# Attention values as split side-by-side tiles, query blocks in pairs, softmax one unit further ahead

## Chip, cores and metric

The program runs on one core of one Trainium2 chip. The metric is the device time of one execution in microseconds. Engines are named as in the profile: PE (matrix products), PEld (its weight loads), DVE, ACT, POOL, SP.

## What is computed

One hybrid layer (a gated MLP mixer, an attention called NSA with 16 heads in 4 groups of 64 columns, a recurrent mixer, a merge, a feed-forward part) on 512 rows of 1024, then two layers of another kind. The change lies in NSA, whose core is, for each head:

```python
s_c = einsum(q, kc) * scale; p_c = softmax(where(valid_c, s_c, NEG))      # compressed keys, 31
o_cmp = einsum(p_c, vc)
p   = softmax(where(kpos <= t, q @ k_slc * scale, NEG));  o_slc = p @ v_slc    # selected blocks
sw  = softmax(where(wmask, q @ k_win * scale, NEG));      o_win = sw @ v_win   # window of 512
o   = g[0] * o_cmp + g[1] * o_slc + g[2] * o_win         # g = sigmoid of 3 gates per head and query
```

With 512 rows there are 8 blocks of 64 and the top 16 are asked for, so that every block is selected, and the window of 512 covers everything: both branches are causal attention over 512 keys, with keys and values of their own. Then `o` is multiplied by a weight matrix.

## The kernel before

All projections are products in fp32r, each operand split into a high part (rounded) and a low part (the rest), with three products of 512 or 280 columns for each pair of tiles. ACT makes the high half of a weight panel (`split_hi`), DVE the low half (`split_lo`); SP loads the next panel when `w_lo` says that the old one was split.

Attention runs over *units*. `unit(u)` gives, for head k = u // 6, six units v = u % 6 (96 in all; k runs over 16 heads): the query block `qb` of 128 rows, the first branch `b` and how many branches `n` (selected, window). v0 is block 0 with both branches, v1 block 1 with both, v2 and v3 block 2 with one branch each, v4 and v5 block 3 with one branch each. A unit goes through:

- `scores(u)` on PE: query block by keys, high and low part (fp32r), and the causal mask by a bf16 product, into bank 4 + u % 2; it waits until the exp of unit u - 2 is done.
- `maxima(u)` on DVE, `exps(u)` on ACT with the row sums (an exp and a read of the accumulator for each branch), `factor(u)` on DVE (reciprocal, times gate), and on POOL (L600) the multiplication of the probabilities `Pn` by that factor; three buffers.
- `transposes(u)` on PE (L2310), one for each 128 keys and branch, into bank 6; the copy to `PTn` by ACT for even u (L981), by DVE for odd u (L1627).
- `values(u)` on PE: for each branch and key block a product of the whole value tile `Vt` (128 columns, two groups of 64, plain fp32, two instructions a product) with 128 columns of `PTn`, added in bank 7. Only the 64 rows of the unit's own group are used. The first unit of a head starts its rows with the compressed branch (31 rows by 512 columns).
- After the sixth unit ACT makes the high part of the output (`o_hi`, L958) and DVE the low part (`o_lo`), from bank 7.

The order is written out by hand. In step u PE does `scores(u + 2)`, some matmuls of the next projection (`fill`, the panel `gmlp_v`, 192 matmuls in all, 52 before the loop and nine a head in it), `transposes(u)`, more `fill`, `values(u - 1)`. ACT does `exps(u + 2)`, for even u the copy, for v0 `o_hi` of the head before; DVE `maxima(u + 2)`, `factor(u + 1)`, for odd u the copy, for v0 `o_lo`. The splits of the filler's weights stand in the same queues, at units found by `slot_after` (1, 30, 62 and 94 or one to two later). All queues are in order. All products are recorded on line 2076 (`mm`).

## Time and profile before

| | before |
|---|---|
| median of 3 runs | 2606.17 us (2605.89 to 2609.31) |
| profiled execution | 2610.13 us, span 2608.5 us |
| PE busy | 2563.4 us (98%), 12825 instructions |
| PEld busy | 2136.6 us (82%) |
| DVE busy | 1201.1 us (46%) |
| ACT busy | 924.1 us (35%) |
| POOL busy | 404.4 us (16%) |
| chain that ended last | PE 92%, DVE 4%, ACT 2%, POOL 1%, DMA 1% |
| granted PE clock | 0.997 of full |

Times in the rows are microseconds from the span's start, or ns where it says mean. In a timeline a row is one or more instructions of a kind in a row: start, length from the first start to the last end, engine, line, operation, output<-inputs, shapes and count; at the end, in brackets, idle time of the engine before it and who ended it. PE overlaps its instructions, so the time that one costs is read from start to start. The loop of the attention runs from 186 to about 407 us.

### The profile page before, as it was taken

The numbers are of one execution on the slowest core, as the hardware profiler recorded it, in microseconds if no ns is written. First come the engines' busy times: TensorE is split into PE (matmuls) and PEld (weight loads), VectorE is DVE, ScalarE is ACT, GpSimd is POOL, SyncE is SP. The second block draws the span as 40 slices with busy tenths as digits, with TensorE's granted clock in tenths as the row PEclk, the third lists the DMA queues.
The fourth block names the chain that finished last, engine by engine and source line by source line (L and its number), as shares of the span: only waits on it lengthen the run. The fifth ranks groups of instructions, "written<-read, shape, count | busy, mean of one in ns | idle before, by whom it ended". The sixth has DMA issues, their size and how long they took to land.

```text
span 2608.5 us, 31776 instructions
## 1 busy us (share of the span) xinstructions
PE 2563.4 (98%) x12825; PEld 2136.6 (82%) x12825; DVE 1201.1 (46%) x1665; ACT 924.1 (35%) x1316; POOL 404.4 (16%) x426
## 2 busy tenths in 40 slices
PE   8999999999999999999999999999999999999998
PEld 7877778887888888888888888888888888888886
DVE  5445553645544574464523333443452333443435
ACT  6435454226323422122533333223253433223232
POOL 2103332300000010000301001321012111022300
PEclk9999999999999999999999999999999999999999
DMA  5220002232242364452233232222223222322231
GB/s 210 81 83 15 17 17 93 97 101 81 81 178 97 127 210 159 150 193 81 81 113 113 97 103 97 87 92 81 97 77 117 97 97 89 127 87 86 88 104 65
DMA packets 58205, 265.49 MB, mean 102 GB/s; under 512 B 5385, under 2 KB 21905, under 8 KB 32865
## 3 DMA queue, kind: packets, MB, share of 16 engines
q1 hardware_dynamic: 46672, 223.39, 25.0%
q0 software_dynamic: 11120, 39.27, 4.3%
q8 instruction: 92, 1.51, 0.2%
q10 hardware_dynamic: 288, 1.05, 0.1%
q14 instruction: 33, 0.26, 0.0%
HBM read 261.60 MB, written 2.10 MB: 101 GB/s over the span
## 4 chain that ended last, share of the span: by engine, by line
PE 92%; DVE 4%; ACT 2%; POOL 1%; DMA 1%; issue 1%; DVEq 0%; SPq 0%; ACTq 0%
PE PS L2076 89%; DVE w_split L1273 1%; PE PS L2310 1%; ACT w_split L699 1%; POOL merged L600 1%; DMA raw<-in_weights 1%; DVE small L1580 1%; PE PS L2498 1%; PE PS L2165 0%; DVE ks_lo L1514 0%; DVE xres L1343 0%; PE PS L2576 0%; ACT merged L878 0%; ACT merged L877 0%; DVE xres L2031 0%
## 5 line engine op out<-in xcount | busy, mean ns | idle before, releaser
L2076 PE MATMUL PS<-h_act,w_split 128*128 128x512 f32 (+1 forms) x5856 | 1268.4, 377 | 12.9 <-DVE w_split L1273 3.9
L2076 PEld LDWEIGHTS PS<-h_act,w_split 128*128 128x128 f32 x5856 | 1048.5, 189 | 214.1 <-DVE w_split L1273 4.7
L1273 DVE TENSOR_TENSOR w_split<-raw,w_split 128x2048 fp32r<-128x2048 f32 x209 | 502.2, 2403 | 832.9 <-ACT w_split L699 819.1
L699 ACT ACTIVATE w_split<-raw 128x2048 fp32r<-128x2048 f32 x209 | 400.2, 1915 | 888.6 <-PE PS L2076 880.3
L2076 PE MATMUL PS<-w_split,h_act 128*128 128x512 f32 (+1 forms) x1920 | 454.4, 387 | 4.5 <-DVE w_split L1273 3.3
L2076 PEld LDWEIGHTS PS<-w_split,h_act 128*128 128x128 f32 x1920 | 349.4, 189 | 67.6 <-DVE w_split L1273 4.3
L2076 PE MATMUL PS<-y_act,w_split 128*128 128x512 f32 x1152 | 263.4, 389 | 0.0
L2076 PEld LDWEIGHTS PS<-y_act,w_split 128*128 128x128 f32 x1152 | 216.3, 188 | 44.9
L2076 PE MATMUL PS<-w_split,y_act 128*128 128x512 f32 x528 | 132.0, 398 | 0.4 <-DVE w_split L1273 0.4
L2076 PE MATMUL PS<-R 128*128 128x128 f32 (+3 forms) x576 | 128.0, 368 | 0.0
L600 POOL TENSOR_TENSOR merged<-merged,small 128x256 f32<-128x256 f32 (+2 forms) x96 | 88.2, 918 | 209.6 <-DVE small L1589 209.2
L2076 PEld LDWEIGHTS PS<-R 128*128 128x128 f32 x576 | 92.4, 191 | 25.3 <-issue 13.9
L2076 PEld LDWEIGHTS PS<-w_split,y_act 128*128 128x128 f32 x528 | 95.5, 188 | 17.7 <-DVE w_split L1273 0.8
L662 POOL TENSOR_TENSOR merged<-merged,cm 128x128 f32<-128x128 f32 (+2 forms) x24 | 41.7, 1764 | 411.0 <-DVE cm L1913 411.0
L950 ACT ACTIVATE merged<-PS,small 128x128 f32<-128x128 f32 (+3 forms) x128 | 66.9, 525 | 108.7 <-DVE small L1580 108.6
L804 ACT ACTIVATE stage<-PS 128x512 f32<-128x512 f32 x94 | 55.9, 598 | 136.8 <-PE PS L2076 136.7
L1580 DVE TENSOR_REDUCE small<-PS 128x2 f32<-128x256 f32 (+2 forms) x96 | 57.7, 601 | 69.8 <-PE PS L2076 69.6
L2076 PE MATMUL PS<-w_split,res_hi 128*128 128x512 f32 x256 | 79.0, 390 | 0.0
L655 POOL TENSOR_TENSOR res_hi<-h_act,cf 128x512 fp32r<-128x512 f32 x16 | 24.5, 1532 | 251.5 <-DVE h_act L1281 251.5
L2076 PEld LDWEIGHTS PS<-merged,R 128*128 128x128 f32 x432 | 53.2, 191 | 7.5 <-issue 6.8
L2076 PE MATMUL PS<-merged,R 128*128 128x128 f32 x432 | 58.6, 278 | 0.1
L2310 PE MATMUL PS<-cf,merged 128*128 128x128 f32 x320 | 51.5, 275 | 6.5 <-POOL merged L600 4.6
(310 smaller groups left out, 2052.6 us busy)
## 6 DMA issues: line engine op xcount, KB each, us to landing
raw<-in_weights SPq DMA_DIRECT2D x197, 1024.0 KB, 4.8
R<-in_w_ada POOLq DMA_DIRECT2D x36, 512.0 KB, 4.9
raw<-in_weights SPq DMA_DIRECT2D x18, 512.0 KB, 4.9
gate_bc<-in_w_ada POOLq DMA_DIRECT2D x12, 512.0 KB, 4.7
raw<-in_weights SPq DMA_DIRECT2D x16, 256.0 KB, 3.6
R<-in_nsa_wk POOLq DMA_DIRECT2D x1, 2048.0 KB, 12.0
xres<-in_x POOLq DMA_DIRECT2D x1, 2048.0 KB, 10.2
R<-in_decay POOLq DMA_DIRECT2D x8, 256.0 KB, 3.3
```

Of the source, the lines that this page charges most:

```text
L600: pool.tensor_tensor(probs, probs, nsa_fac[:, u % 4, 0:n].unsqueeze(2).to_broadcast([P, n, nk]), ALU.mult).then_inc(p_ready, 1)
L655: pool.tensor_tensor(residue_tiles[part][kt].rearrange("p (r i) -> p r i", r=RES), source, ones, ALU.mult).then_inc(residues_ready, 1)
L662: pool.tensor_tensor(probs, probs, share.unsqueeze(2).to_broadcast(list(probs.shape)), ALU.mult).then_inc(a_p, 1)
L699: act.activation(w_split[:, 0, half, :, :], raw[:, half, :, :], ACT.Copy).then_inc(w_hi, 1)
L804: act.activation(stage[:, slot0 + j, :], PS[:, 4 * S + j, :], func).then_inc(staged, 1)
L950: last = act.activation(Pn[:, u % 3, k * nk:(k + 1) * nk], PS[:, 4 + u % 2, k * nk:(k + 1) * nk], ACT.Exp, bias=nsa_nmx[:, u % 4, k:k + 1] ...
L1273: dve.tensor_tensor(w_split[:, 1, half, :, :], raw[:, half, :, :], w_split[:, 0, half, :, :].bitcast(F32), ALU.subtract).then_inc(w_lo, 1)
L1580: dve.reduce_max(nsa_nmx[:, u % 4, 0:n], PS[:, 4 + u % 2, 0:n * (qb + 1) * P] .rearrange("p (b k) -> p b k", b=n), AX, negate=True).then_i ...
L2076: return pe.matmul(out, lhsT, rhs, start=start, stop=stop, skip_group_check=True)
L2310: last = pe.transpose(PS[:, 6, k * P:(k + 1) * P], Pn[:, u % 3, k * P:(k + 1) * P], ident)
L2498: last = pe.transpose(PS[:, 4 * S + b, k * P:(k + 1) * P], tile, ident)
```

## The change

- The unit order within a head becomes block 0, block 1, block 2 branch 0, block 3 branch 0, block 2 branch 1, block 3 branch 1. Units are taken in pairs of query blocks: `chunk(u)` lists which blocks of probabilities of the pair are transposed at step u and which products follow. A product now covers one or two query blocks (128 or 256 columns).
- The stationary value tile holds, for one group and branch, the high half and the low half of the values side by side (64 + 64 columns, fp32r). ACT makes the high, DVE (first group pair) or POOL (second) the low halves.
- The transposed probabilities are split too: ACT makes the high part of every unit (`pt_hi`), DVE the low part (`pt_lo`), from banks 6 and 3 in turn. Each product runs twice, with the high and with the low part.
- Both halves of bank 7 now belong to the same head: ACT copies the other half (`o_other`), DVE adds (`o_sums`), ACT makes the high part (`o_hi`), POOL the low part (`o_lo`). The compressed product fills all 128 rows of bank 7 (its values are padded with zeros to 128 columns) and waits for that sum.
- Scores, maxima and exps run three units ahead instead of two, the factor two instead of one, with a fourth buffer of probabilities. Transposes of even units wait for both units of their pair.
- The filler uses banks 0, 1, 2, 0 and the staggered order; its first weight half is free after 72 of 96 matmuls instead of 48.

The diff, cut to this:

```diff
-    qb, b, n = ((0, 0, 2), (1, 0, 2), (2, 0, 1), (2, 1, 1), (3, 0, 1), (3, 1, 1))[v]
+    qb, b, n = ((0, 0, 2), (1, 0, 2), (2, 0, 1), (3, 0, 1), (2, 1, 1), (3, 1, 1))[v]
...
+def chunk(u):
+    v = u % 6
+    if v == 0:
+        return ([Block(k, (k + 1) * P * b) for b in range(2) for k in range(2)],
+                [Product(0, b, 0, 2, 2 * P * b) for b in range(2)])
+    if v == 1:
+        return [Block(1, 2 * P * b + P) for b in range(2)], [Product(1, b, 1, 2, P * b) for b in range(2)]
+    b = v // 2 - 1
+    if v % 2 == 0:
+        return ([Block(k, P * kb) for kb in range(2) for k in range(2)],
+                [Product(kb, b, 2, 4, 2 * P * kb) for kb in range(2)])
+    return ([Block(0, 2 * P), Block(1, 2 * P), Block(1, 3 * P)], [Product(2, b, 2, 4, 0), Product(3, b, 3, 4, 2 * P)])
...
-assert slot_after(FILL_SIZE // 2 * 3 + 12) > UNITS // 2
+FILL_BANKS = (0, 1, 2, 0)
+FILL_TILE_DONE = (36, 48, 84, 96)
+FILL_HALF_DONE = 72
+assert slot_after(FILL_SIZE + FILL_TILE_DONE[0]) > UNITS // 2 + 1
...
+        def pt_tile(u, part):
+            if u % 2 == 0:
+                return pt_even[:, part, :]
+            return y_act[:, part, 2, :] if u // 6 < 4 else pt_late[:, part, :]
...
+        def v_parts(tiles, g, part):
+            return tiles.rearrange("p t (b g a n) -> p t b g a n", b=2, g=2, a=2)[:, :, :, g, part ^ g, :]
+        def v_both(gp, kb, b, g):
+            tile = V0_pairs[kb // 2][:, kb % 2, :] if gp == 0 else V1_all[:, kb, :]
+            return tile[:, (2 * b + g) * P:(2 * b + g + 1) * P]
...
+                pool.wait_ge(p_ready, products)
+                pool.wait_ge(hi_made, at("att").h + k + 1)
+                rows = slice(64 * (k % 2), 64 * (k % 2) + 64)
+                lo = y_act[rows, 1, k // 2, :]
+                pool.tensor_tensor(lo, y_sum[rows, k // 2, :], y_act[rows, 0, k // 2, :].bitcast(F32), ALU.subtract
+                                   ).then_inc(act_lo, 1)
+                pool.wait_ge(act_lo, at("att").l + k + 1)
             for u in range(UNITS):
                 gp, hp, g, qb, b, n = unit(u)
                 nk = (qb + 1) * P
                 pool.wait_ge(fac_ready, u + 1)
-                probs = Pn[:, u % 3, 0:n * nk].rearrange("p (b k) -> p b k", b=n)
+                probs = probs_tile(u)[:, 0:n * nk].rearrange("p (b k) -> p b k", b=n)
                 pool.tensor_tensor(probs, probs, nsa_fac[:, u % 4, 0:n].unsqueeze(2).to_broadcast([P, n, nk]), ALU.mult
                                    ).then_inc(p_ready, 1)
+                if u % 6 == 4 and u > 6:
+                    o_lo(u // 6 - 1, u + 1)
+                if u == UNITS // 2 - 1:
+                    for g in range(2):
+                        pool.wait_ge(v_ready, 8 + g)
+                        src = Vt1.rearrange("p t (b g n) -> p t b g n", b=2, g=2)[:, :, :, g, :]
+                        pool.tensor_tensor(v_parts(V1_all, g, 1), src, v_parts(V1_all, g, 0).bitcast(F32),
+                                           ALU.subtract).then_inc(v_lo, 1)
+            o_lo(4 * HPG - 1, UNITS)
...
-                act.activation(Vt[gp], banks[:, :, 0:256], ACT.Copy).then_inc(v_ready, 1)
+                if gp == 0:
+                    for t in range(2):
+                        for g in range(2):
+                            src = banks[:, 2 * t:2 * t + 2, 0:256].rearrange("p t (b g n) -> p t b g n", b=2, g=2)
+                            act.activation(v_parts(V0_pairs[t], g, 0), src[:, :, :, g, :], ACT.Copy
+                                           ).then_inc(v_ready, 1)
+                else:
+                    act.activation(Vt1, banks[:, :, 0:256], ACT.Copy).then_inc(v_ready, 1)
                 act.activation(gS[:, gp], banks[:, :, 256:280], ACT.Sigmoid).then_inc(v_ready, 1)
-                release(S, v_ready, 2 * gp + 2)
+                if gp == 1:
+                    release(S, v_ready, 7)
                 split_hi(c.g + 1, 1)
...
-                if u >= 3:
-                    act.wait_ge(t_ready, u - 2)
+                if u >= 4:
+                    act.wait_ge(t_ready, 2 * ((u - 4) // 2) + 2)
                 for k in range(n):
-                    last = act.activation(Pn[:, u % 3, k * nk:(k + 1) * nk], PS[:, 4 + u % 2, k * nk:(k + 1) * nk],
+                    last = act.activation(probs_tile(u)[:, k * nk:(k + 1) * nk], PS[:, 4 + u % 2, k * nk:(k + 1) * nk],
                                           ACT.Exp, bias=nsa_nmx[:, u % 4, k:k + 1],
                                           accum_out=nsa_sum[:, u % 4, k:k + 1])
...
+            def o_other(k):
+                act.wait_ge(o_ps, k + 1)
+                rows, other = [slice(64 * (x % 2), 64 * (x % 2) + 64) for x in (k, k + 1)]
+                act.activation(y_sum[rows, k // 2, :], PS[other, 7, :], ACT.Copy).then_inc(o_part, 1)
             def o_hi(k):
-                act.wait_ge(o_ps, k + 1)
+                act.wait_ge(o_sum, k + 1)
                 rows = slice(64 * (k % 2), 64 * (k % 2) + 64)
-                act.activation(y_act[rows, 0, k // 2, :], PS[rows, 7, :], ACT.Copy).then_inc(hi_made, 1)
+                act.activation(y_act[rows, 0, k // 2, :], y_sum[rows, k // 2, :], ACT.Copy
+                               ).then_inc(hi_made, 1)
+            def pt_hi(u):
+                act.wait_ge(t_ready, u + 1)
+                cols = P * len(chunk(u)[0])
+                act.activation(pt_tile(u, 0)[:, 0:cols], PS[:, (6, 3)[u % 2], 0:cols], ACT.Copy).then_inc(pt_act, 1)
...
-            for u in range(UNITS + 2):
+            exps(2)
+            for u in range(UNITS + 3):
                 if u < UNITS:
-                    gp, hp, g, qb, b, n = unit(u)
-                    if u + 2 < UNITS:
-                        exps(u + 2)
-                    if u % 2 == 0:
-                        act.wait_ge(t_ready, u + 1)
-                        cols = n * (qb + 1) * P
-                        act.activation(PTn[:, u % 2, 0:cols], PS[:, 6, 0:cols], ACT.Copy).then_inc(pt_act, 1)
-                    if u % 6 == 0 and u:
-                        o_hi(u // 6 - 1)
-                if u == UNITS:
-                    o_hi(4 * HPG - 1)
+                    pt_hi(u)
+                    if u + 3 < UNITS:
+                        exps(u + 3)
+                if u % 6 == 0 and 0 < u <= UNITS:
+                    o_other(u // 6 - 1)
+                if u % 6 == 1 and 1 < u:
+                    o_hi(u // 6 - 1)
+                if u == UNITS // 2 - 5:
+                    for g in range(2):
+                        src = Vt1.rearrange("p t (b g n) -> p t b g n", b=2, g=2)[:, :, :, g, :]
+                        act.activation(v_parts(V1_all, g, 0), src, ACT.Copy).then_inc(v_ready, 1)
                 for f in range(FILL_GROUPS):
-                    if u == slot_after(FILL_SIZE * f + FILL_SIZE // 2):
+                    if u == slot_after(FILL_SIZE * f + FILL_HALF_DONE):
                         split_hi(at("gmlp_v").g + f + 1, 0)
                     for j in range(4):
-                        if u == slot_after(FILL_SIZE * f + FILL_SIZE // 2 + 12 * (j + 1)):
+                        if u == slot_after(FILL_SIZE * f + FILL_TILE_DONE[j]):
                             fill_tile(f, j)
                     if u == slot_after(FILL_SIZE * (f + 1)) + 1:
                         split_hi(at("gmlp_v").g + f + 1, 1)
...
-            for gp in range(2):
-                skip(at("nsa.v", gp))
+            c = at("nsa.v", 0)
+            split_lo(c.g + 1, 0)
+            dve.wait_ge(v_ready, 5)
+            for t in range(2):
+                for g in range(2):
+                    src = PS[:, 2 * t:2 * t + 2, 0:256].rearrange("p t (b g n) -> p t b g n", b=2, g=2)
+                    dve.tensor_tensor(v_parts(V0_pairs[t], g, 1), src[:, :, :, g, :],
+                                      v_parts(V0_pairs[t], g, 0).bitcast(F32), ALU.subtract).then_inc(v_lo, 1)
+            release(0, v_lo, 4)
+            split_lo(c.g + 1, 1)
+            skip(at("nsa.v", 1))
...
-            def o_lo(k):
-                dve.wait_ge(hi_made, c.h + k + 1)
+            def o_sums(k):
+                dve.wait_ge(o_part, k + 1)
                 rows = slice(64 * (k % 2), 64 * (k % 2) + 64)
-                low(y_act[rows, 1, k // 2, :], PS[rows, 7, :], y_act[rows, 0, k // 2, :])
+                both = y_sum[rows, k // 2, :]
+                dve.tensor_tensor(both, PS[rows, 7, :], both, ALU.add).then_inc(o_sum, 1)
+            def pt_lo(u):
+                dve.wait_ge(pt_act, u + 1)
+                cols = P * len(chunk(u)[0])
+                dve.tensor_tensor(pt_tile(u, 1)[:, 0:cols], PS[:, (6, 3)[u % 2], 0:cols],
+                                  pt_tile(u, 0)[:, 0:cols].bitcast(F32), ALU.subtract).then_inc(pt_dve, 1)
...
+            maxima(2)
+            factor(1)
             for u in range(UNITS + 3):
+                if u + 3 < UNITS:
+                    maxima(u + 3)
+                if u % 6 == 1 and 1 < u:
+                    o_sums(u // 6 - 1)
+                if u + 2 < UNITS:
+                    factor(u + 2)
                 if u < UNITS:
-                    gp, hp, g, qb, b, n = unit(u)
-                    if u + 2 < UNITS:
-                        maxima(u + 2)
-                    if u + 1 < UNITS:
-                        factor(u + 1)
-                    if u % 2 == 1:
-                        dve.wait_ge(t_ready, u + 1)
-                        cols = n * (qb + 1) * P
-                        dve.tensor_copy(PTn[:, u % 2, 0:cols], PS[:, 6, 0:cols]).then_inc(pt_dve, 1)
-                    if u % 6 == 0 and u:
-                        o_lo(u // 6 - 1)
-                if u == UNITS:
-                    o_lo(4 * HPG - 1)
+                    pt_lo(u)
                 for f in range(FILL_GROUPS):
-                    if u == slot_after(FILL_SIZE * f + FILL_SIZE // 2) + 1:
+                    if u == slot_after(FILL_SIZE * f + FILL_HALF_DONE) + 1:
                         split_lo(at("gmlp_v").g + f + 1, 0)
                     if u == slot_after(FILL_SIZE * (f + 1)) + 2:
                         split_lo(at("gmlp_v").g + f + 1, 1)
...
-                        out = PS[:, 4 * S + bank0 + j, 0:width]
+                        out = PS[:, 4 * S + bank0 + banks[j], 0:width]
+                        if first and j in begin:
+                            begin[j]()
...
-                    yield from dense(at("gmlp_v").plus(C(g=n, u0=n)), 0, Hr, feat=False)
+                    yield from dense(at("gmlp_v").plus(C(g=n, u0=n)), 0, Hr, feat=False, stagger=True, banks=FILL_BANKS,
+                                     begin={3: lambda: pe.wait_ge(gv_raw, 4 * n + 1)})
...
-            def transposed(u):
-                pe.wait_ge(pt_dve if u % 2 else pt_act, u // 2 + 1)
             def transposes(u):
-                gp, hp, g, qb, b, n = unit(u)
-                pe.wait_ge(p_ready, u + 1)
-                if u:
-                    transposed(u - 1)
-                else:
+                pe.wait_ge(p_ready, u // 2 * 2 + 2)
+                if u == 0:
                     pe.wait_ge(pct_act, 4)
-                for k in range(n * (qb + 1)):
-                    last = pe.transpose(PS[:, 6, k * P:(k + 1) * P], Pn[:, u % 3, k * P:(k + 1) * P], ident)
+                blocks = chunk(u)[0]
+                for k, block in enumerate(blocks):
+                    last = pe.transpose(PS[:, (6, 3)[u % 2], k * P:(k + 1) * P],
+                                        probs_tile(u // 2 * 2 + block.unit)[:, block.col:block.col + P], ident)
                 last.then_inc(t_ready, 1)
...
-                gp, hp, g, qb, b, n = unit(u)
+                gp, hp, g = unit(u)[0:3]
                 if u % 6 == 0:
                     rows = slice(32 * hp, 32 * hp + NCMP)
-                    mm(PS[64 * g:64 * g + 64, 7, :], vc[rows, 2 * gp + g, :], PcT[2 * gp + g][rows, :], True, False)
                     if u:
-                        pe.wait_ge(act_lo, att.l + u // 6)
-                transposed(u)
-                nk = (qb + 1) * P
-                for k in range(n):
-                    for kb in range(qb + 1):
-                        last = mm(PS[:, 7, qb * P:(qb + 1) * P], Vt[gp][:, kb, (b + k) * P:(b + k + 1) * P],
-                                  PTn[:, u % 2, k * nk + kb * P:k * nk + (kb + 1) * P], False, True)
+                        pe.wait_ge(o_sum, u // 6)
+                    mm(PS[:, 7, :], vc[rows, 2 * gp + g, :], PcT[2 * gp + g][rows, :], True, False)
+                if u % (UNITS // 2) == 0:
+                    pe.wait_ge(v_lo, 4 + 2 * gp)
+                pe.wait_ge(pt_dve, u + 1)
+                for x in chunk(u)[1]:
+                    n = (x.q1 - x.q0) * P
+                    for part in range(2):
+                        last = mm(PS[:, 7, x.q0 * P:x.q1 * P], v_both(gp, x.kb, x.b, g),
+                                  pt_tile(u, part)[:, x.col:x.col + n], False, True)
                 if u % 6 == 5:
                     last.then_inc(o_ps, 1)
...
+            scores(2)
             for u in range(UNITS):
-                if u + 2 < UNITS:
-                    scores(u + 2)
+                if u + 3 < UNITS:
+                    scores(u + 3)
                 fill((FILL[u] + 1) // 2)
                 transposes(u)
                 fill(FILL[u] // 2)
```

## Rows read from the trace of the kernel before

**Rows 1.** View of windows, the attention: window, length, busy (instructions) of PE, PEld, DVE, ACT, POOL
```profile
186.00:409.00 223.00, 215.85 (x1505) 172.03 (x1504) 125.02 (x351) 112.38 (x324) 88.39 (x97) 1.00 0.05 15
```

**Rows 2.** Timeline of PE in one head: start, length, engine, line, operation, count
```profile
236.10 0.30 PE L2076 MATMUL PS<-ks_hi,qs 128*128 128x128 f32 x1
...
244.38 1.07 PE L2076 MATMUL PS<-R,merged 31*64 31x512 f32 x2
...
245.37 0.71 PE L2076 MATMUL PS<-merged,R 128*128 128x128 f32 x4
...
245.84 0.48 PE L2076 MATMUL PS<-ks_hi,qs 128*128 128x512 f32 x1
...
246.43 0.48 PE L2076 MATMUL PS<-w_split,h_act 128*128 128x512 f32 x1
...
246.75 0.49 PE L2310 MATMUL PS<-cf,merged 128*128 128x128 f32 x3
...
249.72 0.30 PE L2076 MATMUL PS<-ks_hi,qs 128*128 128x128 f32 x1
...
250.29 0.48 PE L2076 MATMUL PS<-w_split,h_act 128*128 128x512 f32 x1
...
250.84 0.66 PE L2310 MATMUL PS<-cf,merged 128*128 128x128 f32 x4
...
251.34 0.83 PE L2076 MATMUL PS<-merged,R 128*128 128x128 f32 x6
...
251.92 0.36 PE L2076 MATMUL PS<-ks_hi,qs 128*128 128x256 f32 x1
...
252.13 0.28 PE L2076 MATMUL PS<-ks_lo,qs 128*128 128x256 f32 x1
...
252.24 0.28 PE L2076 MATMUL PS<-ks_hi,qs 128*128 128x256 f32 x1
```

**Rows 3.** Timeline of ACT, DVE and POOL in the same head
```profile
239.91 0.47 ACT L950 ACTIVATE merged<-PS,small 128x256 f32<-128x256 f32 x1 [1.25 <-DVE small L1580]
...
240.73 0.20 ACT L950 ACTIVATION_READ_ACCUMULATOR merged<-PS,small 128x1 f32 x1
...
246.66 0.69 DVE L1580 TENSOR_REDUCE small<-PS 128x1 f32<-128x512 f32 x1 [0.90 <-PE PS L2076]
...
247.39 0.69 ACT L950 ACTIVATE merged<-PS,small 128x512 f32<-128x512 f32 x1 [1.91 <-DVE small L1580]
...
247.70 0.83 POOL L600 TENSOR_TENSOR merged<-merged,small 128x384 f32<-128x384 f32 x1 [1.63 <-DVE small L1589]
...
247.97 0.19 ACT L950 ACTIVATION_READ_ACCUMULATOR merged<-PS,small 128x1 f32 x1
...
248.71 0.69 DVE L1580 TENSOR_REDUCE small<-PS 128x1 f32<-128x512 f32 x1 [1.09 <-PE PS L2076]
...
249.32 0.15 DVE L1588 RECIPROCAL small<-small 128x1 f32<-128x1 f32 x1
...
249.75 1.04 POOL L600 TENSOR_TENSOR merged<-merged,small 128x512 f32<-128x512 f32 x1 [1.22 <-DVE small L1589]
```

**Rows 4.** Groups by line and form, 186 to 409 us: count, busy, mean ns
```profile
L1281 DVE TENSOR_TENSOR y_act<-PS,y_act 64x512 fp32r<-64x512 f32 x15 | 10.3, 688 | 22.3 <-ACT y_act L958 22.3
...
L981 ACT ACTIVATE merged<-PS 128x512 f32<-128x512 f32 x16 | 9.5, 595 | 0.8 <-PE PS L2310 0.8
```

**Rows 5.** Views of two lines on POOL: shortest, median, longest ns
```profile
L675 POOL TENSOR_TENSOR R<-R x16: 1277/1288/1293, 1598.8 to 2439.7; 128x512 f32<-128x512 f32 x16
...
L677 POOL TENSOR_TENSOR R<-R x16: 1277/2309/3341, 1600.0 to 2440.9; 128x512 f32<-128x512 f32 x16
```

**Rows 6.** Timeline around a weight split inside a head
```profile
259.57 2.54 DVE L1273 TENSOR_TENSOR w_split<-raw,w_split 128x2048 fp32r<-128x2048 f32 x1
...
264.99 0.31 PE L2076 MATMUL PS<-ks_hi,qs 128*128 128x128 f32 x1
```

**Rows 7.** Timeline of PE in the last group ahead of the attention
```profile
147.66 1.55 PE L2076 MATMUL PS<-w_split,h_act 128*128 128x280 f32 x10 [0.96 <-DVE w_split L1273]
```

46 lines of the change are left out of this document (35 added, 11 removed).

## The prediction, made before the changed kernel was built

> **What bounds the kernel now.** The page first: TensorE (PE) is busy for 98% of the span, so only a stretch in which PE has work taken away or is made to wait can change the time. The change touches one stretch, the attention from about 186 to 409 us, and the last weight group ahead of it. The view of windows [rows 1] shows 215.9 us of PE busy in those 223, DVE 125, ACT 112, POOL 88: PE is the bound on average, but this kernel hands every unit through all four engines, so the averages don't decide. I therefore read the timeline of one head (six units, v0 to v5) by the starts of its instructions, since PE's durations overlap. The scores of unit v0 start at 236.10 and again at 249.72 [rows 2]: a head takes 13.62 us. At one place PE is already late: between the projection matmul at 250.29 and the transposes at 250.84 lie 0.55 us, where the same matmul is followed after 0.32 us at 246.43 [rows 2]; 0.23 us of waiting for the probabilities that POOL finishes at 250.79 [rows 3]. So PE's own work in a head is 13.39 us, and the softmax chain stands right behind it.
>
> **What the edit takes from PE.** The values of a head are now 20 products of 128 columns, each of two fp32 instructions; six of these take 0.58 us (251.34 to 251.92), 0.10 each, so 4.0 us a head. After the change they are 24 fp32r instructions of 128 or 256 columns, in blocks of four. The scores show their price: the first of a block 0.21 us, the next 0.11 (251.92, 252.13, 252.24) [rows 2]. Six blocks of 0.21 + 3 x 0.11 make 3.2 us. The compressed product, 0.99 us now (244.38 to 245.37), keeps its 512 fp32 columns; a stationary tile twice as wide is not shown, I bound it by 0.99 and 1.10 and take 1.05. PE's work falls by 0.75 us to about 12.6 us a head. If nothing else counted, 15 heads would give 15 us.
>
> **What it adds to the others.** Per head, with the durations of [rows 4]: ACT converts six transposed tiles instead of copying three (0.60 us for 512 columns) and copies the other 64 rows of the output (taken as the same 0.60). DVE subtracts six tiles (0.69 for 512 columns) instead of copying three, and adds instead of subtracting at the head's end. POOL takes over the low half of the output. Its nearest row is a two-input operation on 512 elements, 1.28 us [rows 5]; its lower bound is the multiplication with a broadcast factor, 1.04 [rows 3]. I take 1.28. In totals the engines still have room (ACT about 8 of 13.6 us, DVE about 9.5, POOL about 7). The question is the order in each queue.
>
> **The chain after the change.** Prices [rows 2 to 4]: transposes of four blocks are readable 0.66 us after their start; ACT starts 0.04 later; an activation lets the next start 0.11 before its end (the accumulator read starts at 247.97, 0.58 into an exp of 0.69), so 0.49 for a copy of 512 and 0.68 for exp of 512; two exps of 256 with their reads last 1.02 (239.91 to 240.93); DVE's maximum starts 0.23 after the scores' block ends (246.43 to 246.66) and lets the next start after 0.61 (248.71 to 249.32); POOL starts 0.43 after the factor's first step (249.32 to 249.75), which I write as 0.35 + 0.08, multiplies for 1.04 (0.83 for 384 columns), PE starts 0.05 later. In the new queues ACT converts transpose u *before* the exps of u+3, DVE takes the maximum of u+3, then (in v1) the output's sum, then the factor of u+2, then the low part of u; even transposes wait for both units of their pair. This closes three links, in time from the transposes of v4:
> - to the transposes of the next v0, which need p(v1): 0.66 + 0.04 + 0.49 (conversion) + 1.02 (exps of v1) = 2.21. DVE is by then still on the low part of v4 (1.34 to 1.94) and the maximum of v2 (to 2.42). Then 0.35 + 0.08 + 1.04 + 0.05 = 3.94. PE's own work up to there is 3.64.
> - on to the values of v0, which overwrite the whole of bank 7 and so wait for the sum of the previous head: 0.70 + 0.49 + 0.68 (exps of v3, ahead in ACT's queue) + 0.60 (other half) + 0.07 (DVE still on the maximum of v4) + 0.69 (sum) + 0.05 = 3.28. PE's own work: 2.86. Before, the compressed product did not have to wait for this; now it stands behind the wait, with everything behind it.
> - on to the transposes of v4, which need p(v5): 1.05 + 0.56 (values v0) + 0.59 (scores of v5, 245.84 to 246.43) + 0.22 + 0.61 (maximum v5, in front of the factor of v4) + 0.35 + 0.08 + 0.83 (p(v4)) + 0.07 + 1.28 (low half of the output, in front of p(v5) on POOL) + 0.07 + 1.04 + 0.05 = 6.80. Without the low half there it would be 6.28, PE's own work being 6.21.
>
> Sum: 3.94 + 3.28 + 6.80 = 14.02 us a head, against 13.62. The 0.75 us freed on PE turn into 1.4 us of waiting. Looking one unit further ahead does not help, because it is ACT's and DVE's queue that hold the next unit back, not the scores.
>
> **The rest of the sum.** Fifteen heads x 0.40 = +6.0. A head in which DVE splits a weight half (2.54 us in its queue) took 264.99 - 249.72 = 15.27, 1.65 more than the others [rows 6]; two such heads lie in the old loop, the third split falling into its first units. In the new order of the filler (half 0 free only after 72 of 96 matmuls) it falls at unit 13, in the running loop: +1.65. POOL's two low parts of the second value pair (2 x 1.28) stand before p(48) and p(49), which are needed later than that: 0 to 2, I take +0.5. In the group ahead of the attention PE already waits 0.96 us for DVE's second half [rows 7]; ACT's four value copies instead of one stand in front of that: 0 to 1, I take +0.5. DVE's four value subtractions there lie beside ACT's own 1.9 us split, at nothing; without that cover they would cost 1.8. The drain gets one hand-over more (conversion, then low part): +0.7. The start, with one unit more in flight but no split in it, -0.4. Sum: 6.0 + 1.65 + 0.5 + 0.5 + 0.7 - 0.4 = +9 us. The profiled execution took 2610.1 us (span 2608.5); it becomes 2619. It is 4 us above the median of the runs, 2606.2, which becomes 2615. A measurement of this kernel can tell about 0.2%, 5.2 us, from no change.
>
> **The rivals.**
> 1. *The chain is shorter than PE's work* (the other side). It decides from 12.6 us a head, that is if 1.4 us of the 14.02 are not there: if DVE and ACT come to each step at once. For it: two of the three links exceed PE's work by under 0.5 us, and their sums use in-order waits that I placed by hand. Against it: the old loop already waits 0.23 us on the same chain with only half the conversions. Then 15 x (12.65 - 13.62) = -14.5, and +2 for the rest: 2593.
> 2. *Only POOL's addition is off*: if the low half finds a gap (an earlier factor for v4), the third link is 6.28 and a head 13.5: 15 x -0.12 = -2, with +3 for the rest: 2607.
> 3. *Splits cost double.* [Rows 5]: the same POOL operation of 512 elements takes 1.28 us in one line and 2.31 (up to 3.34) in the line right behind it, so something beside it can hold POOL up. If each of the three splits also stops POOL's new work, the head loses its 2.3 us and POOL's 1.3: three times +2 more, with some more for the value parts: 2622. The Trainium skill ("SBUF — State Buffer", Who interferes with whom) says that a VectorE instruction with two SBUF inputs and a GpSimd instruction that reads SBUF shut each other out for their whole length. By it the weight split (both inputs in SBUF) is such a partner and the new subtractions from PSUM are not; the sum of this rival comes out of it, that of the forecast is without it. The trace has the long durations, but does not show whose they are.
> 4. *The change doesn't do what it says*: the wide stationary tile loads slower than the narrower shapes of [rows 2], so that PE keeps its 13.4 us of work. The chain still decides, and with PE closer behind it a head is 14.2: 2618.
>
> **How the numbers follow.** Forecast 0.41 (2611 to 2619), rival 1 0.18 (2587 to 2600), rival 2 0.28 (2601 to 2611), rival 3 0.10 (2619 to 2626), rival 4 0.03. Faster by over 0.2% (under 2601): rival 1 and the low end of 2, 0.20. Slower (over 2611.4): forecast, 3 and 4, less 0.04 at the forecast's low end, 0.50. Within: 0.30. The range, 2594 to 2622, leaves out half of rival 1 and half of rival 3, 0.14. It holds the bounds of the prices: 1.04 instead of 1.28 for POOL's addition takes 15 x 0.24 = 3.6 off, the unknown value parts move it by 2.
>
> **What would show it.** In the profile after: values as blocks of four at 0.21/0.11; a head of about 14.0 us; PE idle before the transposes of v0 (0.3) and v4 (0.6), put down to POOL, and before the compressed product (0.4), put down to DVE's sum; POOL's low half between p(v4) and p(v5); three heads of 15.6. A head of 12.6 without waits proves rival 1, one of 13.5 with the wait at v4 gone rival 2. It would be wrong altogether if a 256-column fp32r product in these blocks did not take 0.11, or if the waits stood at other units than these.

## The result and the profile after

The changed kernel takes 2621.7 us (median of four runs, 2619.0 to 2623.0) against 2606.8 for the kernel before, run beside it (2605.9 to 2609.3): a ratio of 1.0052, 95% interval 1.0039 to 1.0064. It is slower, by more than the 0.2% that can be told. The profiled execution took 2623.0 us, its span 2621.4 against 2608.5, so +12.9 where +9 was forecast.

Busy times of the changed kernel, then the view of windows for the attention (columns as in [rows 1]):

```profile
PE 2549.5 (97%) x12569; PEld 2114.4 (81%) x12569; DVE 1235.8 (47%) x1717; ACT 957.1 (37%) x1385; POOL 430.5 (16%) x445
...
186.00:409.00 223.00, 192.41 (x1200) 143.03 (x1199) 152.00 (x387) 138.60 (x378) 105.31 (x108) 0.98 0.04 15
```

Beside [rows 1], in the same 223 us, the other three engines are busier (DVE 152 instead of 125, ACT 139 instead of 112, POOL 105 instead of 88), and PE stands idle for 30.6 us instead of 7.2. The same stretch of the clock isn't the same work, though: after it the changed kernel still has 11 us of attention to do. Up to the first matmul of the next dense part (407.63 us before the change, 420.49 after it) the windows are, before and after:

```profile
186.00:407.63 221.63, 214.48 (x1500) 170.86 (x1498) 123.65 (x351) 111.78 (x323) 87.56 (x95) 1.00 0.05 15
...
186.00:420.49 234.49, 199.64 (x1245) 148.26 (x1244) 157.58 (x399) 144.25 (x388) 109.49 (x112) 0.99 0.04 14
```

For the same work PE is busy for 199.6 us instead of 214.5, so the values did get cheaper, and idle for 34.9 instead of 7.2. The waits from 186 to 430 us name who it waits for (engine, line, tile, releaser: total us, number, longest; the PEld rows are the waits of the weight loads, which run ahead of the products):

```profile
PEld PS L2426 <- POOL merged L678: 15.9, 16, 3.2
...
PEld PS L2426 <- POOL R L678: 12.2, 12, 1.8
PE PS L2426 <- POOL merged L678: 10.8, 15, 2.9
PE PS L2195 <- DVE y_sum L1711: 9.2, 15, 0.6
PE PS L2426 <- POOL R L678: 8.5, 12, 1.6
```

L2426 is the transposes, waiting for POOL's probabilities; L2195 here is the compressed product, waiting for the output sum of the previous head, once a head for 0.6 us. One head on PE's timeline, from the transposes of v4 to the next ones, shows the three waits of the forecast, each at its place:

```profile
242.76 0.33 PE L2426 MATMUL PS<-cf,merged 128*128 128x128 f32 x1 [0.74 <-POOL R L678]
...
246.69 0.66 PE L2426 MATMUL PS<-cf,merged 128*128 128x128 f32 x4 [0.29 <-POOL merged L678]
...
250.04 1.12 PE L2195 MATMUL PS<-R,merged 31*128 31x512 f32 x2 [0.62 <-DVE y_sum L1711]
251.09 0.74 PE L2195 MATMUL PS<-pt_even,v_early 128*128 128x256 f32 x4
251.67 0.40 PE L2195 MATMUL PS<-ks_hi,qs 128*128 128x512 f32 x1
...
256.89 0.66 PE L2426 MATMUL PS<-cf,merged 128*128 128x128 f32 x4 [0.75 <-POOL merged L678]
```

The links are 246.69 - 242.76 = 3.93 us, 3.35 and 6.85, together 14.13. Without the three waits (0.29, 0.62 and 0.75 us) PE's own work in this head is 12.46 us. The same head on POOL and DVE:

```profile
240.22 1.28 POOL L669 TENSOR_TENSOR y_act<-y_sum,y_act 64x512 fp32r<-64x512 f32 x1
241.67 1.04 POOL L678 TENSOR_TENSOR R<-R,small 128x512 f32<-128x512 f32 x1 [0.16 <-DVE small L1705]
...
239.08 0.16 DVE L1705 TENSOR_TENSOR small<-small,R 128x1 f32<-128x1 f32 x1
...
240.77 0.76 DVE L1705 TENSOR_TENSOR small<-small,R 128x1 f32<-128x1 f32 x1
```

L669 is the low half of the output, in POOL's queue ahead of p(v5), as foreseen. Not foreseen is DVE's factor beside it: one number a row, 0.16 us in the unit before, here 0.76. It ends at 241.53, when L669 ends (241.50).

The starts of v0's scores give all heads of the trace: 13.45, 14.12, **18.55**, 14.12, 14.25, **15.75**, 14.11, 14.39, five of 14.11 to 14.13, **15.76**. The three in bold hold a weight split on DVE. The last two cost 1.63 and 1.64 us, as forecast, the first 4.43. There, on DVE and POOL, and PE afterwards:

```profile
221.70 2.28 DVE L1380 TENSOR_TENSOR w_split<-raw,w_split 128x2048 fp32r<-128x2048 f32 x1
...
224.42 0.70 DVE L1705 TENSOR_TENSOR small<-small,R 128x1 f32<-128x1 f32 x1
...
221.69 3.42 POOL L669 TENSOR_TENSOR y_act<-y_sum,y_act 64x512 fp32r<-64x512 f32 x1
225.26 1.04 POOL L678 TENSOR_TENSOR merged<-merged,small 128x512 f32<-128x512 f32 x1 [0.16 <-DVE small L1705]
```

```profile
219.60:226.30 6.70, 3.87 (x32) 3.31 (x30) 6.07 (x12) 3.13 (x9) 5.28 (x3) 0.98 0.16 35
226.30:232.70 6.40, 6.34 (x25) 5.15 (x26) 2.74 (x7) 2.56 (x8) 1.66 (x3) 0.50 0.31 129
232.70:239.10 6.40, 5.81 (x35) 4.04 (x33) 3.56 (x12) 3.40 (x9) 1.87 (x2) 0.99 0.00 0
```

The low half starts beside the split and ends at 225.11: it takes 2.14 us more than its own 1.28, nearly the whole length of the split (2.28). PE then waits 2.9 us (the longest wait above), and for the next 6.4 us its granted clock is 0.50, that is 1.2 GHz instead of 2.4.

The time lost, part by part. Both traces start the same transposes at 181.25, so that they can be laid on each other from there:

- the start, up to the second head's first scores: 14.30 us before, 11.84 now, -2.5 (before the change the first split stood here, and PE waited 1.59 us behind it);
- 14 heads at 0.50 more: +7.0;
- what stands out of the row of heads (the splits, the low parts of the second values), 7.4 us now against 2.9 before: +4.5;
- the drain, from the last head's first scores to the next dense part: 18.51 us before (389.12 to 407.63), 22.30 now (398.19 to 420.49), +3.8;
- behind the drain the clock is at 0.50 for about 3 us, in the dense part: +1.6.

That is 14.4 us in all; the same matmuls of the dense part behind lie 14.46 us apart in the two traces. The span grew by only 12.9 because 1.5 us come back around 1250 us, far behind the change; experiment 9's trace gains the same 1.5 us there, so it is the trace of the kernel before that is slow at that place. The drain, with the four waits that make it longer:

```profile
413.49 0.74 PE L2195 MATMUL PS<-pt_even,v_both 128*128 128x256 f32 x4 [0.66 <-DVE pt_even L1716]
...
415.86 0.33 PE L2426 MATMUL PS<-cf,merged 128*128 128x128 f32 x1 [1.62 <-POOL R L678]
...
417.93 0.74 PE L2195 MATMUL PS<-pt_even,v_both 128*128 128x256 f32 x4 [0.66 <-DVE pt_even L1716]
...
419.97 0.68 PE L2195 MATMUL PS<-pt_late,v_both 128*128 128x256 f32 x4 [1.31 <-DVE pt_late L1716]
...
421.00:424.00 3.00, 3.00 (x9) 2.35 (x8) 1.81 (x2) 0.90 (x2) 0.36 (x1) 0.51 0.28 44
```

### The profile page after: what moved, and what is told of

Same layout as the page of the kernel before. It is cut to its first block, busy times and chain, and to the rows that moved or that the text cites. A ratio compares the mean times of both kernels' runs of the same rounds, so it can differ in the third digit from the quotient of the medians.

```text
span 2621.4 us, 31327 instructions
## 1 busy us (share of the span) xinstructions
PE 2549.5 (97%) x12569; PEld 2114.4 (81%) x12569; DVE 1235.8 (47%) x1717; ACT 957.1 (37%) x1385; POOL 430.5 (16%) x445
## 3 DMA queue, kind: packets, MB, share of 16 engines
q10 hardware_dynamic: 288, 1.05, 0.1%
## 4 chain that ended last, share of the span: by engine, by line
PE 88%; DVE 5%; ACT 3%; issue 2%; POOL 1%; DMA 1%; DVEq 0%; SPq 0%; POOLq 0%; ACTq 0%
PE PS L2195 85%; DVE w_split L1380 1%; PE PS L2426 1%; POOL merged L678 1%; ACT pt_even L1064 1%; ACT w_split L786 1%; DVE small L1705 1%; DVE small L1696 1%; DMA raw<-in_weights 1%; PE PS L2618 0%; POOL R L678 0%; DVE y_sum L1711 0%; ACT y_sum L1053 0%; PE PS L2286 0%; DVE ks_lo L1621 0%
## 5 line engine op out<-in xcount | busy, mean ns | idle before, releaser
L2195 PE MATMUL PS<-h_act,w_split 128*128 128x512 f32 (+1 forms) x5856 | 1269.6, 377 | 12.2 <-DVE w_split L1380 3.1
L2195 PEld LDWEIGHTS PS<-h_act,w_split 128*128 128x128 f32 x5856 | 1049.4, 189 | 213.8 <-issue 4.9
L2195 PE MATMUL PS<-w_split,h_act 128*128 128x512 f32 (+1 forms) x1920 | 455.3, 388 | 3.9 <-DVE w_split L1380 2.9
L2195 PEld LDWEIGHTS PS<-w_split,h_act 128*128 128x128 f32 x1920 | 350.3, 189 | 67.0 <-DVE w_split L1380 4.0
L2195 PE MATMUL PS<-y_act,w_split 128*128 128x512 f32 x1152 | 263.4, 389 | 0.0
L2195 PEld LDWEIGHTS PS<-y_act,w_split 128*128 128x128 f32 x1152 | 216.2, 188 | 44.9
L2195 PE MATMUL PS<-w_split,y_act 128*128 128x512 f32 x528 | 132.0, 398 | 0.4 <-DVE w_split L1380 0.4
L2195 PE MATMUL PS<-R 128*128 128x128 f32 (+3 forms) x576 | 128.0, 368 | 0.0
L2195 PEld LDWEIGHTS PS<-R 128*128 128x128 f32 x576 | 92.4, 191 | 25.3 <-issue 13.9
L2195 PEld LDWEIGHTS PS<-w_split,y_act 128*128 128x128 f32 x528 | 95.5, 188 | 17.7 <-DVE w_split L1380 0.8
L678 POOL TENSOR_TENSOR merged<-merged,small 128x384 f32<-128x384 f32 (+2 forms) x72 | 61.3, 852 | 158.8 <-DVE small L1705 158.6
L2195 PE MATMUL PS<-w_split,res_hi 128*128 128x512 f32 x256 | 79.0, 390 | 0.0
L1696 DVE TENSOR_REDUCE small<-PS 128x1 f32<-128x384 f32 (+1 forms) x96 | 57.1, 595 | 28.2 <-PE PS L2195 26.8
L2426 PE MATMUL PS<-cf,merged 128*128 128x128 f32 x224 | 44.1, 285 | 20.5 <-POOL merged L678 10.8
L723 POOL DMA_DIRECT2D R<-in_w_ada x36 | 19.1, 532 | 241.1 <-DVEq L1907 241.1
L1246 ACT ACTIVATE R<-PS 128x512 f32<-128x512 f32 x48 | 28.7, 598 | 79.8 <-PE PS L2195 79.8
L1064 ACT ACTIVATE pt_even<-PS 128x512 fp32r<-128x512 f32 x48 | 28.7, 598 | 79.7 <-PE PS L2426 79.7
```

The costliest lines, as they stand in the source:

```text
L678: pool.tensor_tensor(probs, probs, nsa_fac[:, u % 4, 0:n].unsqueeze(2).to_broadcast([P, n, nk]), ALU.mult).then_inc(p_ready, 1)
L1064: act.activation(pt_tile(u, 0)[:, 0:cols], PS[:, (6, 3)[u % 2], 0:cols], ACT.Copy).then_inc(pt_act, 1)
L1246: act.activation(dst, src, ACT.Copy, scale=scale).then_inc(qk_ready, 1)
L1696: dve.reduce_max(nsa_nmx[:, u % 4, 0:n], PS[:, 4 + u % 2, 0:n * (qb + 1) * P] .rearrange("p (b k) -> p b k", b=n), AX, negate=True).then_i ...
L2195: return pe.matmul(out, lhsT, rhs, start=start, stop=stop, skip_group_check=True)
L2426: last = pe.transpose(PS[:, (6, 3)[u % 2], k * P:(k + 1) * P], probs_tile(u // 2 * 2 + block.unit)[:, block.col:block.col + P], ident)
```

## The experiments

Each kernel is the changed kernel with the edit shown, unless it says otherwise. Head lengths are distances between starts of v0's scores in its trace.

**1. The low half of the output on GpSimd two units later.**

```
-                if u % 6 == 4 and u > 6:
-                    o_lo(u // 6 - 1, u + 1)
+                if u % 6 == 0 and u > 6:
+                    o_lo(u // 6 - 2, u + 1)
...
+            o_lo(4 * HPG - 2, UNITS)
             o_lo(4 * HPG - 1, UNITS)
```

> POOL makes the low half of the output one head later, behind the probabilities of v0, where POOL stands idle for 2 us, instead of between those of v4 and v5. Theory (the chain through the queues sets the head): the transposes of v4 no longer wait for it. In the changed kernel the factor of v5 was held from 240.93 to 241.53 and the transposes of v4 began at 242.76; without it 240.93 + 0.08 + 1.04 + 0.05 = 242.10, so a head of 14.12 - 0.66 = 13.5 us, and 15 x 0.66 = 9.9 us off the time. The head with the first weight split, 18.55 us, loses more, since low half and split no longer meet: 15.5 or less, another 2 us off. Together 2609 to 2611. Rival (PE's own work decides, or another queue has taken the bound): the head stays at 14.1 and only the split's head gets shorter, 2619.

Measured: 2610.3 us (2608.5 to 2619.6), ratio to the kernel before 1.0014 (1.0005 to 1.0024); heads of 13.52. In a head of this trace the wait at v4 is gone, the other two stand:

```profile
345.09 0.33 PE L2427 MATMUL PS<-cf,merged 128*128 128x128 f32 x1 [0.34 <-POOL R L678]
...
348.45 1.12 PE L2196 MATMUL PS<-R,merged 31*128 31x512 f32 x2 [0.60 <-DVE y_sum L1712]
```

One position in one queue is worth 0.60 us a head, and 11.4 us of the 14.9 lost: 9 in the heads, and 2 in the head of the first split (16.54 instead of 18.55), where the low half no longer lies beside it. The same trace shows a new event: at unit 47 the two low parts of the second values (2.51 us in POOL's queue) now lie close to a low half of the output. PE waits 1.87 us, and the clock is at 0.50 for some 13 us behind it; the heads there take 18.21 and 15.59. The profiled execution is the longest of ten (2619.6), and the others lie between 2608.5 and 2613.4. So this fall of the clock probably doesn't come in every execution; only the profiled one has a trace.

**2. The first halves' splits two units later.**

```
-                    if u == slot_after(FILL_SIZE * f + FILL_HALF_DONE):
+                    if u == slot_after(FILL_SIZE * f + FILL_HALF_DONE) + 2:
```

(on ScalarE, and the same + 2 on VectorE)

> The splits of the filler's first weight half stand two units later in ACT's and DVE's queue (at v3 and v4 instead of v1 and v2 for the first, v2 and v3 for the second); nothing else moves. Theory (DVE's split and POOL's low half of the output shut each other out when they meet, and the pause of 2.9 us on PE then costs the clock): the first split's head falls from 18.55 to about 15.8 us, as the other two have it (15.75), and PE's clock does not fall: 2.8 us off the time, 2618 to 2619. Rival (a split at this point of the loop costs 4.4 us because the loop has no slack left, whoever is beside it): the head stays between 17.5 and 19, no change. All other heads stay at 14.12.

Measured: 2622.2 us, ratio 1.0053 (1.0036 to 1.0070): nothing gained. Moving the split away from the low half does end the mutual hold-up (on POOL 1.28 us again, the head 17.41 instead of 18.55), but PE still waits 2.49 us and the clock still falls to 0.50, for about 3 us instead of 6.4. And the split of unit 30, a second half, which the edit doesn't touch, got dearer, a head of 17.96 instead of 15.75:

```profile
271.18 0.47 PE L2426 MATMUL PS<-cf,merged 128*128 128x128 f32 x1 [1.23 <-POOL R L678]
```

that is the same 1.23 us of idle time as in the changed kernel's trace, only that the clock fell behind it here, for 6.6 us, and not there:

```profile
271.00:277.60 6.60, 6.42 (x26) 5.23 (x27) 2.91 (x10) 2.56 (x8) 1.77 (x3) 0.51 0.02 7
```

So a stretch of the loop at half the clock costs some 2.2 us (17.96 - 15.75). And my theory, the hold-up, covers at most 1.1 of the first split's 4.4 us, since the low clock got shorter in the same run. An estimate of the 4.4: 1.6 for the split in DVE's queue, as in the other two heads, 2.2 for the clock (from the head of 17.96), and 0.6 left for the hold-up and whatever else is different at this unit.

**3. Exponentials ahead of the conversion on ScalarE.**

```
                 if u < UNITS:
-                    pt_hi(u)
                     if u + 3 < UNITS:
                         exps(u + 3)
+                    pt_hi(u)
```

> ACT takes the exps of unit u + 3 before it converts the transposes of u, instead of behind. Theory of the prediction, taken at its word (the second link is set by DVE too: the low part and the maximum stand in front of the output's sum): the exps come 1 us earlier but the conversions 0.1 to 0.2 later, and DVE reaches the factor of v1 and the output's sum at the same time as before; a head stays within 14.0 to 14.3, the time within 2618 to 2624. Rival (ACT's order alone holds the chain): the factor of v1 and the sum come 0.5 us earlier each, a head of 13.3, 12 us off, 2610.

Measured: 2659.5 us, ratio 1.0198 (1.0181 to 1.0215). Both expectations missed it; a head takes 17.0 us. The order that the prediction blames for the lack of lead is far better than its opposite. Waits from 300 to 400 us:

```profile
ACT merged L1045 <- DVE small L1696: 28.8, 22, 3.2
DVE pt_even L1716 <- ACT pt_even L1064: 20.6, 18, 1.3
ACT R L1045 <- DVE small L1696: 14.1, 8, 3.0
```

ACT now waits for the maxima of u+3 with the conversion of u behind them, DVE's low part waits for the conversion, and the values for both. And each head now holds a stall of 1.2 to 1.4 us ahead of the compressed product, behind which the clock is low:

```profile
342.00:346.00 4.00, 4.00 (x18) 3.16 (x17) 0.92 (x3) 1.02 (x3) 1.13 (x2) 0.57 0.02 4
```

**4. PE's work in the values halved** (the products with the low parts of the probabilities are left out; their conversion stays).

```
-                    for part in range(2):
+                    for part in range(1):
```

> The products with the low part of the probabilities are left out (12 of 24 products a head, half of the values' work on PE); the low parts are still made and waited for. Theory (chain): PE loses 12 x 0.11 = 1.3 us of work a head, but only the products of v0 lie in the chain, so that a head falls by 0.2 to 0.3 us only, to 13.8 to 13.9, 4 us off, 2617. Rival (PE's work decides): a head of 12.8, 20 us off, 2602.

Measured: 2616.6 us (2616.3 to 2622.2), ratio 1.0038 (1.0024 to 1.0052); head 13.88. Some 1.5 us of PE's work a head are gone (half of six blocks of 0.41 to 0.58) and 0.24 us come back, as the theory said: the head is not PE's. What PE no longer does it waits, for example 0.98 us at v4 instead of 0.75:

```profile
340.43 0.65 PE L2426 MATMUL PS<-cf,merged 128*128 128x128 f32 x4 [0.98 <-POOL merged L678]
```

**5. The splits in quarters**, one in each of four successive units, on ScalarE and VectorE.

```
+            def split_lo_part(g, half, q):
+                if q == 0:
+                    dve.wait_ge(w_hi, 2 * g + half + 1)
+                ins = dve.tensor_tensor(w_split[:, 1, half, q, :], raw[:, half, q, :],
+                                        w_split[:, 0, half, q, :].bitcast(F32), ALU.subtract)
+                if q == 3:
+                    ins.then_inc(w_lo, 1)
```

> The changed kernel, with the three weight splits that fall into the attention loop (2.28 us each on VectorE, and one operation on ScalarE) cut into four quarters that are issued in four successive units. Theory (a split costs because it stands whole in VectorE's queue, and the first one pushes TensorE into a stall of 2.9 us behind which its granted clock is 0.50 for 6.4 us): the quarters of 0.6 us fit into VectorE's idle times of 0.4 to 1.8 us, so the heads of 18.55, 15.75 and 15.76 us come down to 14.1 to 14.6, no stretch of the loop has the clock at 0.50, and the kernel takes 2621.7 - 4.2 - 2 x 1.4 = 2615 us. Rival (what matters is the sum of VectorE's work between two links, wherever it lies): four units are delayed by 0.6 us each, the three heads stay near 16, only the clock comes back, 2619.

Measured: 2621.3 us, ratio 1.0048 (1.0033 to 1.0064): the heads are on the rival's side. The first split's head falls to 16.24 but its neighbour rises to 14.68, the other two take 15.41 and 16.98. The clock doesn't come back either, against both expectations: behind a wait of 1.20 us in the first head and one of 1.31 in the last it is at 0.50 for some 3 us. A quarter alone would be some 0.6 us (2.28 / 4); the first three on DVE took 0.81, 0.88 and 1.41. The last line is POOL's product beside the third:

```profile
227.13 0.81 DVE L1399 TENSOR_TENSOR w_split<-raw,w_split 128x512 fp32r<-128x512 f32 x1
...
229.38 0.88 DVE L1399 TENSOR_TENSOR w_split<-raw,w_split 128x512 fp32r<-128x512 f32 x1
...
231.84 1.41 DVE L1399 TENSOR_TENSOR w_split<-raw,w_split 128x512 fp32r<-128x512 f32 x1
...
231.66 1.04 POOL L678 TENSOR_TENSOR merged<-merged,small 128x512 f32<-128x512 f32 x1 [1.95 <-DVE small L1726]
```

POOL's products around the three quarters end at 227.39, 229.71 and 232.70, and each quarter ends 0.55 us behind that (227.94, 230.26, 233.25), whenever it had started. So in this trace a quarter waits for the product beside it and then takes its own 0.55. DVE comes to a quarter 0.3 to 0.9 us after it has handed a factor to POOL, while POOL's product runs.

**6. The output sum earlier**: the copy ahead of the exponentials on ScalarE, the addition ahead of the maxima on VectorE.

```
                 if u < UNITS:
                     pt_hi(u)
-                    if u + 3 < UNITS:
-                        exps(u + 3)
                 if u % 6 == 0 and 0 < u <= UNITS:
                     o_other(u // 6 - 1)
+                if u + 3 < UNITS:
+                    exps(u + 3)
...
-                if u + 3 < UNITS:
-                    maxima(u + 3)
                 if u % 6 == 1 and 1 < u:
                     o_sums(u // 6 - 1)
+                if u + 3 < UNITS:
+                    maxima(u + 3)
```

> The changed kernel, with the summing of the two halves of a head's output issued earlier: on ScalarE the copy of the other half ahead of the exponentials of that unit instead of behind them, on VectorE the addition ahead of the maxima. Theory (the second link of the head's chain, from the transposes of v0' to its values, contains the exponentials that stand ahead of the copy): the idle time of 0.62 us before the compressed product goes, each head takes 13.5 us instead of 14.12, the kernel 2621.7 - 15 x 0.6 = 2612.7. Rival (the head is set by VectorE's and GpSimd's row of factors and probabilities, and the exponentials that now come 0.6 us later delay them by as much): the wait moves ahead of the transposes and the head stays at 14.1, 2621.

Measured: 2615.2 us, ratio 1.0029 (1.0018 to 1.0040). Heads of 13.46 and 13.55, as the theory said, and no wait is left ahead of the compressed product. Of the 9 us only 6.5 arrive, because the heads with splits lose some back (17.09, 16.30, 17.89); in each of them the clock falls to 0.50, in the last for 6.8 us, where the changed kernel's trace has it in the first alone.

**7. Four edits together**: 1, 5 and 6, and the low halves of the second values in units 44 and 45 instead of both in 47.

```
-                if u == UNITS // 2 - 1:
-                    for g in range(2):
+                for g in range(2):
+                    if u == UNITS // 2 - 4 + g:
                         pool.wait_ge(v_ready, 8 + g)
```

> Four edits together: the low half of a head's output on GpSimd two units later (as tried alone before: head 13.52, kernel 2610.3), the output sums issued earlier, the splits in quarters, and the low halves of the second values in two units with free time on GpSimd (units 44 and 45 instead of both in 47). Theory (each acts on another link of the chain, so that the gains add up): head 13.52 - 0.6 = 12.9, 15 x 0.6 = 9 less; splits 7 less; no clock at 0.50 within the loop; 2610.3 - 16 = 2594, faster than the kernel before by 0.5%. Rival (behind the waits TensorE's own work is longer than was counted, or a new wait takes the place of each that goes): head 13.4, 2603 to 2606, no difference to the kernel before that can be told.

Measured: 2600.1 us (2597.0 to 2601.5), ratio 0.9967 (0.9955 to 0.9979), faster than the kernel before. The gains of edits 1 and 6 add up: heads of 12.86 and 12.96. The splits' heads are still 13.62 and 13.56 (the first), 14.95 and 15.64, together 6 us, by which the forecast of 2594 was missed. In the last of them PE waits 1.55 us and the clock is at 0.50 for 3.4 us, which the theory had ruled out.

**8. One part undone: the low half of the output on VectorE**, behind the low parts of v1', as before the change.

```
-                if u % 6 == 4 and u > 6:
-                    o_lo(u // 6 - 1, u + 1)
...
+                if u % 6 == 1 and 1 < u:
+                    o_lo(u // 6 - 1)
```

(the first on GpSimd, the second on VectorE)

> The changed kernel, with one part undone: the low half of a head's output is made on VectorE again, behind the low parts of the probabilities of v1', instead of on GpSimd between the products p(v4) and p(v5). Theory (the 1.28 us on GpSimd between the two products is the term of the second and third link, and VectorE is idle for 1.5 us at the place where the step now goes): the idle times before the transposes of v0' and v4 shrink as they did when the step stayed on GpSimd two units later, the head takes 13.5 us, the kernel 2610 to 2612. Rival (the step needs both of its inputs from SBUF, and shuts VectorE and GpSimd out from each other wherever it runs): it takes 1.3 to 1.8 us on VectorE, the factor behind it comes late, head 13.9 to 14.1, 2617 to 2621.

Measured: 2610.5 us (2607.1 to 2612.5), ratio 1.0012 (1.0003 to 1.0021); heads of 13.46, as short as in experiment 1. It takes 1.13 us on DVE in twelve of sixteen heads, with POOL's product beside it (0.69 in the others), in a gap, and costs nothing there:

```profile
344.63 1.13 DVE L1376 TENSOR_TENSOR y_act<-y_sum,y_act 64x512 fp32r<-64x512 f32 x1 [0.20 <-ACT y_act L1046]
...
346.25 0.69 DVE L1684 TENSOR_REDUCE small<-PS 128x1 f32<-128x512 f32 x1 [0.49 <-PE PS L2190]
```

**9. Kernel 7 with the low quarters of the splits on GpSimd**, behind the products of units 20, 21, 26, then 38, 39, 44, then 86, 87, 92 (two quarters in the first unit of each three).

```
+                        ins = pool.tensor_tensor(w_split[:, 1, half, q, :], raw[:, half, q, :],
+                                                 w_split[:, 0, half, q, :].bitcast(F32), ALU.subtract)
```

> The kernel with the four edits together (2600.1), with one step changed: the low quarters of the weight splits run on GpSimd, behind the products of units that leave it 1.35 to 2.54 us free, instead of on VectorE, where each quarter took 0.7 to 1.4 us instead of 0.6 because GpSimd's product stood beside it. Theory (a quarter costs what it holds up in the row maxima, factors, product): a quarter takes 1.28 us on GpSimd and lies in free time, the heads of 13.62, 13.56 and 14.95 us come down to 13.0, that of 15.64 to 14, the kernel takes 2600.1 - 0.65 - 0.65 - 2.0 - 1.5 = 2595. Rival (a quarter on GpSimd shuts VectorE's low parts or factors out for as long): the same three heads stay above 13.5, 2600.

Measured: 2593.0 us (2592.3 to 2594.0), ratio 0.9947 (0.9933 to 0.9960), the fastest of all. The heads are 12.81 to 12.97, but for one of 13.42, in which a quarter and both low parts of the second values stand in POOL's queue; none stands out for a split. POOL around one of them, and the windows of the attention:

```profile
223.92 0.83 POOL L678 TENSOR_TENSOR merged<-merged,small 128x384 f32<-128x384 f32 x1 [0.70 <-DVE small L1730]
224.71 2.51 POOL L689 TENSOR_TENSOR w_split<-raw,w_split 128x512 fp32r<-128x512 f32 x2
227.31 1.04 POOL L678 TENSOR_TENSOR merged<-merged,small 128x512 f32<-128x512 f32 x1
```

```profile
186.00:372.00 186.00, 178.94 (x1132) 132.54 (x1131) 131.01 (x358) 130.91 (x363) 109.10 (x111) 1.00 0.04 12
```

PE is idle for 7.1 us of these 186, and the clock is full throughout. Against the trace of the kernel before, the loop starts 4.9 us earlier, its 14 heads take 181.4 us instead of 193.6 (the splits in them included), and the drain takes 1.6 longer: 15.5 us less for the attention, where the medians differ by 14.0. The starts of the loop lie at 189.8 to 193.2 us in the traces of the changed kernel and its variants with three units of lead, so a part of the 4.9 is scatter.

**10. One part undone: the softmax two units ahead instead of three**, the pairs kept.

```
-                    if u + 3 < UNITS:
-                        exps(u + 3)
+                    if u + 2 < UNITS:
+                        exps(u + 2)
```

(and so for scores, maxima and factors)

> The changed kernel, with one part undone: scores, maxima, exponentials and factors run two units ahead of the transposes again instead of three; the pairs of query blocks stay. Theory (since the transposes of an even unit now need the product of the next unit too, the row from scores over maxima, exponentials, factor to product of 3.3 us has only one unit of TensorE's work, 2.3 us, to hide behind, three times a head): at least 3 x 1 = 3 us more a head, 17 us, more where the clock falls behind the stalls, the kernel 2667 us or more. Rival (the lead was no limit, the head is held by the output's steps alone): head 14.1, 2622 us.

Measured: 2739.6 us, ratio 1.0503 (1.0487 to 1.0519). The theory's side, but far more of it: heads of 20.7 to 24.0. PE waits 1.6 to 1.8 us for POOL at each pair, where I had put 1:

```profile
334.17 0.66 PE L2423 MATMUL PS<-cf,merged 128*128 128x128 f32 x4 [1.64 <-POOL merged L678]
...
339.53 0.33 PE L2423 MATMUL PS<-cf,merged 128*128 128x128 f32 x1 [1.83 <-POOL R L678]
...
331.01:351.82 20.81, 15.19 (x80) 11.59 (x80) 8.84 (x26) 9.38 (x27) 6.65 (x8) 0.83 0.00 0
```

The last line is one head: a mean granted clock of 0.83, so a third of it runs at half speed. With pairs the third unit of lead is necessary; it just doesn't yield more than that.

## Why the prediction was right

**The direction and the mechanism.** PE's own work fell as costed: a block of four values of 256 columns takes 0.58 us (251.09 to 251.67), the compressed product 1.05 (250.04 to 251.09), and the head's own work is 12.46 us where 12.6 was forecast. The forecast was that a chain over the other engines decides instead, and that is shown three ways: halving the values' products gives 0.24 us a head (experiment 4), moving single steps out of the chain gives 0.6 to 0.7 a head each (1, 8, 6), and taking out two gives 1.2 (7).

**The links.** Forecast 3.94 + 3.28 + 6.80 = 14.02, measured 3.93 + 3.35 + 6.85 = 14.13. The third link's 0.52 us for the low half was too small: its removal gave 0.60. Part of that is DVE's factor, which takes 0.76 instead of 0.16 us beside it, so that p(v5) starts 0.17 us behind the low half where 0.07 was put; that term was missing in the sum. Heads: forecast +6.0 in 15, measured +7.0 in 14.

**The splits.** Forecast 1.65 us for the one that moves into the running loop, measured 4.43 (the two others 1.63 and 1.64, as before in [rows 6]). This is one of the two terms that were mis-sized. Rival 3 had named a piece of it, the mutual hold-up of DVE's split and POOL's low half; the trace shows it as 3.42 us for a 1.28 us operation. This agrees with what the Trainium skill ("SBUF — State Buffer", Who interferes with whom) says of a VectorE instruction with two SBUF inputs beside a GpSimd instruction that reads SBUF. But it happened at one split of three and is worth at most 1.1 us (experiment 2; in experiments 1 and 8, where the low half doesn't lie beside the split either, the first split still costs 3.0 us, with the clock at 0.50 for some 3). The larger piece, by the estimate there 2.2 us, is the granted clock of 0.50 behind the stall, which stands in neither the forecast nor a rival. The trace of the kernel before did hold such a case, ahead of its loop: a wait of 2.49 us with the clock at 0.50 behind it.

```profile
172.31 0.47 PE L2076 MATMUL PS<-ks_hi,qs 128*128 128x128 f32 x1 [2.49 <-DVE R L1571]
...
173.00:177.00 4.00, 4.00 (x16) 3.42 (x17) 2.52 (x3) 2.97 (x9) 0.00 (x0) 0.50 0.00 0
```

What it couldn't show is that the loop would stall that long: there its longest waits are 1.59 and 1.68 us, at full clock.

**Start and drain.** This is the other mis-sized term, and it was hidden by a sum. Forecast -0.4 for the start and +0.7 for the drain, together +0.3; measured -2.5 and +3.8, and 1.6 more behind the drain for the clock, together +2.9. The forecast had one more hand-over in the drain. The trace has four waits of 0.66, 1.62, 0.66 and 1.31 us one after the other: with no scores left to do, PE has nothing to put beside the last conversions. No experiment changes the drain by itself, so its cause is read from the trace alone; experiment 9, the fastest, still has one of 20.1 us.

**The small terms.** The low parts of the second values: forecast +0.5, measured 0.27 (a head of 14.39). The last group ahead of the attention: forecast +0.5. The wait that was there [rows 7] shrank to 0.60, and by 181.25 both traces are at the same point, but this term can't be told: v0's first scores start at 172.31 before and 173.74 after, and anywhere between 170.5 and 173.6 in experiments that changed nothing ahead of them.

**The sum.** Forecast +9, measured +14.5 in the traces up to the next dense part: +3.4 from the loop (1.0 of it from the heads, the rest from the first split), +2.6 from start and drain, -0.5 from the last group. The medians say the same: 2621.7 is 14.9 us over the 2606.8 run beside it. So the miss is nearly 6 us of 15, and 2621.7 lies 0.3 us inside the range, outside the 2611 to 2619 that the prediction gave its own forecast and inside the 2619 to 2626 of rival 3. The rival gets its number by a hold-up at each of three splits, which didn't happen. That the time still fell into the stated range is partly luck: the start's gain of 2.1 us over its forecast hid nearly half of what drain and clock cost over theirs. In its working the prediction also takes the rest of the sum as +2 in rival 1 and +3 in rival 2, where its own terms add up to 2.95; rival 1 would be 2595.

**The other rivals.** Rival 1 (12.6 a head) was not what the change did, but it is near where the kernel ends when the chain is put in order: 12.9 in experiments 7 and 9. Rival 2 (13.5 a head, 2607) is what experiments 1 and 8 do: 13.5 and 2610, with the split's cost on top. Rival 4 found nothing for it: PE's own work is 12.46 us a head, not 13.4.

**Looking further ahead.** The prediction says that looking one unit further ahead doesn't help. Against what PE saves by the pairs that is right, the head is still 14.1; but without the third unit a head takes 21 to 24 us (experiment 10), so the pairs need it.

**What the change was worth.** Its saving on PE was real, and was spent in the queues of the other three engines. With the low half of the output, the output sum, the second values' low parts and the splits placed where nobody waits behind them, the same arithmetic takes 2593.0, 0.53% less than the kernel before. Still open is what edit 5 and the moved second values are each worth inside kernel 7, since they were not run alone beside edits 1 and 6, and what a better drain would give.

## What to carry to other kernels

When an edit takes work off the bounding engine and gives it to engines with "room", write down the in-order queue of each of them for one period and add up the links between two waits of the bounding engine; here that gave 14.02 us for a measured 14.13, where PE's own work gave 12.6. Do the same for the loop's first and last period: the drain, with no later unit's work to hide behind, cost 3.8 us where 0.7 was put. Then look for each inserted step at what stands directly behind it in its queue, and move it to where that engine waits anyway: two such moves were worth 0.6 us a head each. Long, rare operations (a 2.3 us weight split in a loop whose slack is under 1 us) are to be placed as carefully as the loop itself, on the engine with the longest gap, and cutting them up didn't help where every piece lay in the row that decides (experiment 5).

## What the runs showed of the hardware

- **A stall can cost twice.** Behind some PE stalls of 1.2 to 2.9 us the granted clock was 0.50: for 6.4 us behind 2.9 us in the changed kernel, some 13 us behind 1.87 in experiment 1; in experiment 10, with a stall of 1.6 to 1.8 us at every pair, the mean over a head was 0.83. Experiment 9, which waits at most 1.2 us inside the loop, kept 1.00 there. The length of one stall alone doesn't decide: the same 1.23 us was followed by the low clock in experiment 2 (2.2 us for the head) and not in the changed kernel, the kernel before has two waits of 1.59 and 1.68 us at full clock, and behind the same wait of 2.49 us ahead of the loop the clock was low for some 6.5 us before the change and 3.4 after it. So what a stall costs can't be read from its length in these traces.
- **A tiny operation can be held up by a large one.** DVE's product of one number a row took 0.76 us instead of 0.16 beside POOL's low half, and 0.70 behind the split, where it again ended with the low half (225.12 and 225.11); DVE's quarters, 0.55 us by themselves, took 0.8 to 1.4 beside POOL's products; POOL's 1.28 us took 3.42 beside DVE's split. DVE operations with one input from PSUM (the low parts of the probabilities) kept their length beside the same POOL work: those of 512 columns took 0.68 to 0.69 us in all 48 cases of the attention.
